# The first block's two projections as products of rounded high and low parts

## What is computed

```python
h = modulate(x, norm1_g[l], shift1, scale1)
proj = h @ w_in[l]
q_g, k_g, v_g, a_lr, r_g, q_s, k_s, v_s = jnp.split(proj, split_at, axis=-1)
log_a = jax.nn.log_sigmoid((a_lr @ w_gla_alpha[l] + b_gla_alpha[l])) / GLA_GATE_TEMP
...
y = jnp.concatenate([o_gla, o_swa], axis=-1) @ w_out[l]
x = x + gate1[:, None, :] * y
h2 = modulate(x, norm2_g[l], shift2, scale2)
```

## Time and profile before

| | us |
|---|---|
| median of three runs | 2934.55 |
| the profiled execution | 2936.04 |
| its span | 2934.3 |
| PE (TensorE matmul) busy | 2243.6 |
| DVE (VectorE) busy | 1422.6 |
| POOL (GpSimd) busy | 1090.0 |
| ACT (ScalarE) busy | 590.1 |

### The profile page before, as it was taken

The page is one execution under the profiler, slowest core; times in us unless marked ns, Lnnn a source line. Parts: engine busy times, 40 slices in busy tenths (PEclk is TensorE's granted clock), DMA queues, the critical chain, the costliest instruction groups (busy, mean ns, idle before and its releaser), DMA issues. The chain is left out here.

```text
span 2934.3 us, 22359 instructions
## 1 busy us (share of the span) xinstructions
PE 2243.6 (76%) x7307; PEld 1264.4 (43%) x7307; DVE 1422.6 (48%) x3566; ACT 590.1 (20%) x1136; POOL 1090.0 (37%) x746
## 2 busy tenths in 40 slices
PE   4896697691677677777777777777778997868899
PEld 1344343481222233222232232222556785745687
DVE  1106541325987767886787766565233111254111
ACT  1202231210000000000000000000444444444443
POOL 1000000131444444444443444443523885601687
PEclk8897698895799999999999999999877998969999
DMA  6200151324999999999999999997522664500465
GB/s 216 52 15 0 48 182 58 102 71 146 375 420 420 420 420 420 420 420 420 413 411 420 405 413 420 420 420 326 160 72 65 179 180 157 159 1 16 149 181 157
DMA packets 174778, 715.05 MB, mean 244 GB/s; under 512 B 18465, under 2 KB 71756, under 8 KB 109132
## 3 DMA queue, kind: packets, MB, share of 16 engines
q0 software_dynamic: 73728, 536.90, 44.3%
q1 hardware_dynamic: 90752, 168.71, 18.5%
q10 hardware_dynamic: 10190, 8.12, 0.9%
HBM read 701.86 MB, written 11.82 MB: 243 GB/s over the span
## 5 line engine op out<-in xcount | busy, mean ns | idle before, releaser
L1504 PE MATMUL ps<-uv_ring_g,expert_diag_g 128*128 128x512 f32 x2048 | 975.3, 624 | 408.0 <-DVE expert_diag_g L1391 407.8
L1283 POOL DMA_INDIRECT uv_ring_g<-in_peer_uv_dram,expert_idx x512 | 574.7, 1122 | 793.9 <-PE ps L1504 692.6
L1504 PEld LDWEIGHTS ps<-uv_ring_g,expert_diag_g 128*128 128x128 f32 x2048 | 385.1, 196 | 997.5 <-DVE expert_diag_g L1391 573.0
L1444 DVE CUSTOM_DVE_ANT_0 uv_ring_g<-uv_ring_g,x_rows 128x1024 f32<-128x1024 f32 x512 | 626.4, 1224 | 332.8 <-DMA uv_ring_g<-in_peer_uv_dram,expert_idx 329.9
L1604 POOL TENSOR_TENSOR w_low_b<-w_raw_b,w_high_b 128x1024 fp32r<-128x1024 f32 x98 | 234.7, 2397 | 236.7 <-ACT w_high_b L1598 235.4
L1604 POOL TENSOR_TENSOR w_low_a<-w_raw_a,w_high_a 128x1024 fp32r<-128x1024 f32 x98 | 234.6, 2396 | 189.7 <-ACT w_high_a L1598 188.4
L1487 ACT ACTIVATE expert_gelu_g<-expert_dot_g 128x2 f32<-128x2 f32 x256 | 52.1, 203 | 1235.7 <-DVE expert_dot_g L1444 1235.7
L271 POOL TENSOR_TENSOR peerq_low<-peerq_raw,peerq_high 128x1024 fp32r<-128x1024 f32 x16 | 38.0, 2380 | 566.8 <-ACT peerq_high L260 566.8
L1391 DVE TENSOR_SCALAR expert_diag_g<-ident,expert_weight_g 128x128 f32<-128x128 f32 x512 | 126.4, 303 | 9.1
L1598 ACT CAST w_high_b<-w_raw_b 128x1024 fp32r<-128x1024 f32 x98 | 102.8, 1051 | 119.3 <-PE ps L1617 119.3
L1598 ACT CAST w_high_a<-w_raw_a 128x1024 fp32r<-128x1024 f32 x98 | 102.8, 1051 | 117.7 <-PE ps L1617 117.7
(11 more groups left out here) (439 smaller groups left out, 3088.5 us busy)
## 6 DMA issues: line engine op xcount, KB each, us to landing
w_raw_a<-in_w_gu_dram SPq DMA_DIRECT2D x44, 512.0 KB, 3.6
w_raw_b<-in_w_gu_dram SPq DMA_DIRECT2D x44, 512.0 KB, 3.6
wada_rest<-in_w_ada_dram SPq DMA_DIRECT2D x16, 1024.0 KB, 5.2
w_raw_a<-in_w_in_dram SPq DMA_DIRECT2D x24, 512.0 KB, 3.9
w_raw_b<-in_w_in_dram SPq DMA_DIRECT2D x24, 512.0 KB, 3.7
w_raw_a<-in_w_down_dram SPq DMA_DIRECT2D x22, 512.0 KB, 3.6
w_raw_b<-in_w_down_dram SPq DMA_DIRECT2D x22, 512.0 KB, 3.6
wada<-in_w_ada_dram SPq DMA_DIRECT2D x4, 2048.0 KB
```

The lines of the kernel that those rows point to most:

```text
L1283: pool.indirect_dma_start(out=self.ring[:, n % self.RING, :], out_offset=None, in_=K.uv, in_offset=bass.IndirectOffsetOnAxis(ap=K.idx[self ...
L1444: dve.tensor_tensor_reduce(u, u, self.h[b][:, :], 1.0, 0.0, ALU.mult, ALU.add, self.a[:, s:s + 1]).then_inc(self.s_dot, 1)
L1504: ins = nc.tensor.matmul(self.bank(half), self.diag[q % self.DIAGS][:, :], self.ring[:, n % self.RING, D + 512 * half:D + 512 * half + 512 ...
```

## The change

The weights of both projections are laid out on the host as contiguous tiles of [128, 1024] (512 KB): for the input, 16 column tiles in the order q/k (4), gate rank (padded to 128 columns), r and q (8), doubled keys (2), window values (1), and 4 tiles of two k each for the values of the gated attention in row form; for the output, 8 column tiles. A new class `Columns` loads them one by one on SyncE's queue into three raw buffers, casts on ScalarE, subtracts on GpSimd, and makes three products each. `Projections` is gone.

```diff
+class Columns:
+    def loads(self, sp):
+        for n, src in enumerate(self.src):
+            if n >= self.RAW:
+                sp.wait_ge(self.s_lo, n - self.RAW + 1)
+            sp.dma_start(self.raw[n % self.RAW][:, :], src).then_inc(self.s_land[n % self.RAW], 16)
+
+    def high(self, act, n):
+        if n >= len(self.src):
+            return
+        act.wait_ge(self.s_land[n % self.RAW], 16 * (n // self.RAW + 1))
+        if n >= self.SPLIT:
+            act.wait_ge(self.s_used, n - self.SPLIT + 1)
+        act.copy(self.hi[n % self.SPLIT][:, :], self.raw[n % self.RAW][:, :]).then_inc(self.s_hi, 1)
...
+    def turned(self, pe, n, bank, x, cols=P):
...
+        pe.wait_ge(self.s_lo, n + 1)
+        for k in range(KD):
+            last = split_product(self.K.nc, bank, (hi[:, k, 0:cols], lo[:, k, 0:cols]), x(k), k == 0, k == KD - 1)
+        last.then_inc(self.s_used, 1)
```

```diff
         @block.scalar
         def _(act):
-            act.dma_start(wnat[:, :, 0:512], wv[:, :, COL_VG:COL_VG + 512]).then_inc(s_wn, 16)
-            act.dma_start(wnat[:, :, 512:640], wv[:, :, COL_VS:COL_VS + P]).then_inc(s_wn, 16)
...
+            act.dma_start(K.wal[:, :], I["w_gla_alpha"][0]).then_inc(s_wal, 16)
             nm.squares(act)
+            w.high(act, 0)
             nm.root(act)
-            nm.shift(act)
+            for n in range(1, w.SPLIT):
+                w.high(act, n)
+            for k in range(KD):
+                act.wait_ge(nm.s_out, k + 1)
+                act.activation(hi[:, k, :], K.hT[:, k, :], ACT.Identity, bias=shift[k]).then_inc(s_hh, 1)
+            for n in range(VG):
+                if out(n)[0] is s_ea:
+                    act.wait_ge(w.s_used, n + 1)
...
+                w.high(act, n + w.SPLIT)
+            w.high(act, VG + w.SPLIT)
         @block.tensor
         def _(pe):
             nm.sums(pe)
+            pe.wait_ge(s_hl, KD)
+            for n in range(VG):
+                if n >= 2:
+                    pe.wait_ge(*out(n - 2))
...
+                    w.turned(pe, n, K.ps[n % 2][:, :], x)
...
+            for c in range(KD // 2):
+                w.rows(pe, VG + c, [K.ps[3 + b][:, :] for b in range(TB)], 2 * c, x)
...
         @block.vector
         def _(dve):
             nm.scale(dve)
+            for k in range(KD):
+                dve.wait_ge(s_hh, k + 1)
+                dve.scalar_tensor_tensor(out=lo[:, k, :], in0=K.hT[:, k, :], scalar=shift[k],
+                                         in1=hi[:, k, :].bitcast(F32), op0=ALU.add, op1=ALU.subtract).then_inc(s_hl, 1)
...
+            dve.wait_ge(w.s_used, VG + KD // 2)
+            for b in range(TB):
+                dve.tensor_copy(K.vg[:, b, :], K.ps[3 + b][:, :]).then_inc(s_vr, 1)
```

In the two attentions the scalings go:

```diff
-            ch.link(dve.tensor_scalar(q, q, GLA_DK ** -0.5, None, ALU.mult))
...
-                if i == 0:
-                    pe.wait_ge(s_q, 1)
...
-            dve.tensor_scalar(q, q, HD ** -0.5, None, ALU.mult).then_inc(s_q, 1)
```

The output stage:

```diff
+        w = Columns(K, ctx, "out1", [I["w_out_1"][n] for n in range(KD)])
+        mix = SplitTiles(K, ctx, "mix", [K.mixT[:, k, :] for k in range(KD)])
         @block.tensor
         def _(pe):
-            pr.products(pe, lambda k: K.mixT[:, k, :], 2, 0)
+            pe.wait_ge(mix.s_lo, KD)
+            for n in range(KD):
+                if n >= 4:
+                    pe.wait_ge(s_x, n - 3)
+                w.turned(pe, n, K.ps[n % 4][:, :], mix)
             nm.sums(pe)
         @block.scalar
         def _(act):
-            nm.squares(act, [(pr.s_free[k % 2], 2 + k // 2) for k in range(KD)])
+            mix.high(act)
+            for n in range(w.SPLIT):
+                w.high(act, n)
+            for n in range(KD):
+                w.high(act, n + w.SPLIT)
+                act.wait_ge(s_x, n + 1)
+                act.activation(K.hT[:, n, :], K.xres[:, n, :], ACT.Square).then_inc(nm.s_sq, 1)
             nm.root(act)
             nm.shift(act)
```

More of the change, by code:

```diff
@@ L167, in ready @@
         return (self.s_shift, len(self.dst)) if self.shifts else (self.s_out, len(self.dst))
[L170 to L218, removed]
 class SplitProjections:
@@ L509, in stage_in1, with out, x @@
     nc, I = K.nc, K.i
+    QK, A, RQ, KS, VS, VG = 0, 4, 5, 13, 15, 16
     with ExitStack() as ctx:
[L511 to L514, removed]
+        w = Columns(K, ctx, "in1", [I["w_in_1"][n] for n in range(VG + KD // 2)])
+        hi = K.sb(ctx, "h_high", [P, KD, S], F32R)
+        lo = K.sb(ctx, "h_low", [P, KD, S], F32R)
+        vT = K.sb(ctx, "swa_valuesT", [P, S])
         rs = K.sb(ctx, "rs1", [P, S])
         nm = Norm(K, "n1", [K.xres[:, k, :] for k in range(KD)], [K.hT[:, k, :] for k in range(KD)], D,
[L517 to L524, removed]
[L525 removed]
+                  [K.g1[:, k:k + 1] for k in range(KD)], K.ones[:, :], K.ps[2][:, :], rs[:, :])
+        shift = [K.modT[:, M_SHIFT1 + k:M_SHIFT1 + k + 1] for k in range(KD)]
+        s_hh, s_hl = K.sem("h_rounded"), K.sem("h_split")
+        s_ea, s_ed = K.sem("columns_out_act"), K.sem("columns_out_dve")
+        s_wal, s_z, s_ze = K.sem("gate_weights_landed"), K.sem("gate_done"), K.sem("gate_out")
+        s_vt, s_vr, s_pad = K.sem("swa_values_turned"), K.sem("value_rows_out"), K.sem("pads_zeroed")
+        block = ctx.enter_context(nc.Block())
+        def out(n):
+            on_dve = [A, KS, KS + 1, VS]
+            return (s_ed, on_dve.index(n) + 1) if n in on_dve else (s_ea, n + 1 if n < A else n)
+        def x(k):
+            return hi[:, k, :], lo[:, k, :]
         @block.sync
         def _(sp):
[L529 to L530 removed]
+            w.loads(sp)
         @block.gpsimd
@@ L590, in _ @@
-            last.then_inc(s_z, 1)
+            pe.wait_ge(s_hl, KD)
+            for n in range(VG):
+                if n >= 2:
+                    pe.wait_ge(*out(n - 2))
+                if n == A:
+                    w.turned(pe, n, K.ps[n % 2][0:RANK, :], x, RANK)
+                else:
+                    w.turned(pe, n, K.ps[n % 2][:, :], x)
+                if n == RQ + 1:
+                    pe.wait_ge(*out(A))
+                    pe.wait_ge(s_wal, 16)
+                    for t in range(2):
+                        last = mm(nc, K.ps[2 + 5 * t][:, :], K.wal[:, t * P:(t + 1) * P], K.alrT[:, :])
+                    last.then_inc(s_z, 1)
@@ L2616 @@
     inputs["w_gu"] = _tiles(_np, _np.concatenate([gate.reshape(D, -1, 256), up.reshape(D, -1, 256)], axis=2).reshape(D, -1))
+    w = inputs.pop("w_in")[0]
+    keys = [w[:, COL_KS + 64 * (g // 2):COL_KS + 64 * (g // 2) + 64] for g in range(2 * SWA_KV)]
+    rank = _np.concatenate([w[:, COL_A:COL_A + RANK], _np.zeros((D, P - RANK), w.dtype)], axis=1)
+    inputs["w_in_1"] = _np.concatenate(
+        [_columns(_np, _np.concatenate([w[:, COL_QK:COL_QK + 512], rank, w[:, COL_RQ:COL_RQ + 1024], *keys,
+                                        w[:, COL_VS:COL_VS + P]], axis=1)),
+         _tiles(_np, w[:, COL_VG:COL_VG + 512]).reshape(-1, P, D)])
+    inputs["w_out_1"] = _columns(_np, inputs.pop("w_out")[0])
     for name in ("w_in_2", "w_out_2", "w_down_2"):
```

131 lines of the change are left out of this document (68 added, 63 removed).

## The result

The changed kernel takes **2888.99 us** (median of four runs, 2887.51 to 2889.68), the kernel before, run beside it, 2934.06 (2932.90 to 2935.36): 0.9847 of it, with a 95% interval of 0.9834 to 0.9859. That is 45.1 us less, where the prediction had 52.1 less; the time lies in the predicted range, near its slow end.

The account below looks back on a forecast made before the run. The prediction saw serial stages before the DMA-bound gather, the input stage having a serial head and Tensor-bound products. Input stage -40.8, scaling -1.2 and output stage -10.1 gave -52.1 us, median 2882.5; range 2874 to 2891.

Parts of the forecast that it names:

- The head: Input stage: without seven Scalar-queue issues, squares start at 57.0, 19.0 us earlier; products start at 81.95, not 96.60.
- signs of a wrong step: Profile after: products waiting for w_low, scalings well over 5.4 us, or squares later than 58 would each prove one.
- so I take 0, and as the other end one full subtraction, 2.4 us: Input stage head: GpSimd's weight subtraction costs Vector operations reading two SBUF tensors nothing, at most 2.4 us.
- The products: Input stage: 16 column tiles, four value tiles, gate matmuls, transposes and slow start run from 81.95 to 197.05.
- neither 5.49 nor 5.60: Time per tile of 24 products: 5.49 us for column tiles, 5.60 for the four value tiles, against 6.86 before.
- the 2.0 taken: Start of the products in the input and output stages: 2.0 us added for running at 1.2 GHz.
- The rival of the passes at the fp32 rate: Products: a tile takes 5.15 us, 10 us less in all, 2872.5; chance 3%.
- The rival in which cast, subtraction and products run one after another: Edited stages: each of 28 tiles costs 3.4 us more, 95 us in all, 2978; chance 3%.
- The output stage: Output projection: products start 7.75 us after the load and take 45.9; the stage ends 10.1 us sooner.
- The scalings: Scalings of q leave Vector: -1.2 us in the gated attention, 0 in the window attention (other end -1.2).
- Everything behind shifted by 52 as one piece: Profile after: all work behind the edited stages moves 52 us earlier together.
- allowance of 4 to 5 us: Whole kernel: margin on either side for another layout of tensors and code, above all for the gather.

Follow-up runs that it names:

- Experiment 3: The kernel before, with the seven weight issues moved from Scalar's queue to SyncE's: 2912.93 us, ratio 0.9932.
- experiment 1: The changed kernel with all three first weight tiles cast on Scalar before the root of the norm: 2881.22 us, ratio 0.9824.
- the changed kernel again: A kernel identical to the changed one, measured and profiled once more: 2889.03 us, ratio 0.9847.
- Experiment 4: The changed kernel with the output stage of the kernel before (fp32 products, loads of 256 columns): 2899.82 us, ratio 0.9885.
- experiment 5: The changed kernel with both scalings of q back as Vector instructions: 2887.10 us, ratio 0.9842.
- experiment 2: The changed kernel with weight tiles 1 and 2 cast between Scalar's shifts, putting two subtractions under Vector's scalings and low parts: 2886.54 us, ratio 0.9838.
- Experiment 6: The changed kernel with one more unused memset ahead of the gated attention's own: 2885.02 us with 512 columns, 2889.18 with 2048.

## Why the prediction was right, and where it was short

**The head** was right in its mechanism: squares 0.41 after the stage's start (0.36 predicted), the weight tile in time. Experiment 3 shows that the queue was the cause. Two of the prediction's own signs of a wrong step are there even so, squares later than 58 (58.44) and a scaling chain over 5.4 (7.42). The first is the stage's start, below. In the head two terms were off. The step "so I take 0, and as the other end one full subtraction, 2.4 us" failed: the term measured 2.03 us. The row it was taken from the earlier trace rows shows Vector's dot product beside GpSimd's indirect DMAs, and GpSimd's subtraction, which reads SBUF itself, is another kind of work. The rule weighed against it, of the Trainium skill (SBUF — State Buffer, section Who interferes with whom), is what the runs bear out, with 2.0 to 2.1 us for each collision and 2.78 against 0.74 us for the instruction that meets one. Against that, 9.29 us passed from the first square to the root and not 9.96, 0.7 better than assumed, since the clock rose earlier under the sums. That is luck: with the same products and squares it was 10.15 in experiment 1 and 9.54 in the changed kernel again.

**The start of the stage** was taken as fixed at 56.64. It was 58.03 in the changed kernel and 56.84 to 58.47 in the experiments, 57.79 in the one with the setup and products of before. It is there already where the setup waits for its third load, shown above; no run was made to find out why that wait ends later. It is 1.4 us of what is missing.

**The products** were right to 1%: 114.05 us from 84.61 to the last, 115.1 predicted. Two errors went against each other. A tile takes 5.44 us in both stages, also written out and for the value rows (0.2267 a matmul), so neither 5.49 nor 5.60 was the figure. The row of the two tiles held it: between the loop's turns its steps are 0.2267 too, and a turn adds 0.1 to the two. Why the feed-forward, with its 0.2333, is slower than the value rows, whose form it has, no run shows. The slow start costs more than the 2.0 taken: the first eviction comes 92.58 - 84.61 = 7.97 after the first product, 2.5 more than a warm tile, and in the output stage 436.84 - 428.41 = 8.43, 3.0 more. The rival of the passes at the fp32 rate is out: three products cost 5.44 / 6.86 = 0.79 of a full one. The four passes of the Trainium skill (FP8 and Floating Point Precision, section TensorE Precision Notes) would make it 0.75. The rival in which cast, subtraction and products run one after another is out too: behind the third tile GpSimd starts each subtraction 1.6 us after an eviction, needs 2.40 and sits idle for about 3 us before the next, and no product waits for it.

**The output stage** was right: products 7.94 after the first load (7.75 predicted), 46.5 from there to the last eviction (45.9 predicted, the difference being the slow start), the stage 9.3 us shorter. Experiment 4 gives 8.4 of it back.

**The scalings.** In the gated attention the scaling was worth 0.74 us and not 1.2 (experiment 5). In the window attention the earlier scores were waited for again, as argued:

```profile
312.21 1.22 PE L110 MATMUL ps<-kTd,rqT 64*128 64x256 f32 x4 [16.92 <-PEq L633]
...
317.83 5.39 PE L110 MATMUL ps<-wada_rest,cact 128*1 128x256 f32 x16 [2.32 <-DMA wada_rest<-in_w_ada_dram]
```

The first modulation waits 2.32 us for its load, where it waited 0.97. That the whole stretch is 1.4 shorter is no gain of the scaling. It is in the sums of the norm at its end, which take 6.75 us before and 5.12 after, the same eight matmuls (before, then after):

```profile
443.44 6.75 PE L110 MATMUL ps<-mixT,ones 128*128 128x512 f32 x8 [2.93 <-ACT mixT L139]
```
```profile
407.31 5.12 PE L110 MATMUL ps<-mixT,ones 128*128 128x512 f32 x8 [2.90 <-ACT mixT L139]
```

From its first load to that of the output stage the window attention takes 109.7 us before and 108.3 after. It takes 109.7 in experiment 2, with no scaling in it, as in experiment 5, with it; and in experiment 3, whose window attention is that of before, scaling and all, it takes 108.1, with the sums at 5.13:

```profile
425.47 5.13 PE L110 MATMUL ps<-mixT,ones 128*128 128x512 f32 x8 [2.91 <-ACT mixT L139]
```

**"Everything behind shifted by 52 as one piece"** is the step that failed most. The gather and the second half did shift as one piece (0.1 and 0.7 us off), but the gated attention grew by 3.6, the largest part of the shortfall. The prediction's allowance of 4 to 5 us was for another layout of tensors and code, and that it held the number is luck, for the cause was another: the same work met the changes of the granted clock at another place. Experiment 6 speaks for this: with a shift of 0.7 us the 3.6 were gone, with 2.3 us most of them were back. Why the new input stage put the attention on the long side stays open.

The sum, in spans: predicted -52.1; +1.4 the start, +2.0 the collision, -0.7 the sums, -0.8 the products and their tail, +3.6 the gated attention, -1.4 the window attention, +0.8 the output stage, +0.8 the rest. That gives -46.4, and the spans say -46.5.

## What to carry to other kernels

Look first at what stands ahead of the first useful instruction on each queue: nearly half of this gain was seven DMA issues in front of eight squares. If a subtraction on GpSimd and an operation of Vector with two SBUF inputs can be kept apart in time by changing the order on a third engine, do it; 2 us each is worth a look. And where the granted clock goes up and down within a stage, as in the attentions here, an edit in one stage can move another by 3 to 5 us either way, as it did here; repeat the kernel with a dummy delay before putting such a difference down to the edit.

## What the runs showed of the hardware that was not expected

- The gated attention's time when only its start is shifted against the work before it: 90.78, 87.21 and 90.24 us with a shift of 0, 0.7 and 2.3 us, one profile each for the last two. The second block's attention did the same once, 89.15 against 93.4 to 94.0. What sets the moments at which the clock changes was not looked for.
- A Vector instruction that begins while GpSimd's subtraction runs took 2.78 us instead of 0.74, and the subtraction kept its 2.35 us: it had begun 0.11 us before, and Vector waited. The reciprocal, with one input in SBUF, kept its 3.35 us beside the same kind of subtraction.
- In the two edited stages products of rounded parts run at one pace, 5.44 us for 24 matmuls of 512 columns at full clock, whether the weights or the rows are stationary; in the feed-forward of the second block it is 5.60.
